# Router products taken from the residual rows, slot matrices built several tiles at a time, and two weight transfers issued behind the first gather

## What is computed

```
xn = rms_norm(x, norm_mix);  x = x + token_mixer(xn, ...)     # attention + gated linear attention
hn = rms_norm(x, norm_ffn)
g_logits = hn @ w_rg + b_rg      # 4 groups, top 1
e_logits = hn @ w_re + b_re      # 8 experts in the group, top 2
out += (silu(hn @ w_gate[e]) * (hn @ w_up[e])) * weight @ w_down[e]
x = rms_norm(x + out, norm_final)
```

## Time and profile before

| what | value |
|---|---|
| median of 3 runs | 623.91 us (623.71 to 625.61) |
| the profiled execution | 623.14 us |
| its span, first to last instruction | 621.4 us |
| granted TensorE clock, mean of the span | 0.99 |
| busy PE / DVE / ACT / POOL | 584.4 / 268.0 / 209.2 / 65.6 us |
| chain that ended last: PE / DMA / SP's queue / DVE | 76 / 11 / 5 / 5% |
| moved by DMA | 155.83 MB, 251 GB/s over the span |

### The profile page before, as it was taken

The page is one execution under the profiler, slowest core; times in us unless marked ns, Lnnn a source line. Parts: engine busy times, 40 slices in busy tenths (PEclk is TensorE's granted clock), DMA queues, the critical chain, the costliest instruction groups (busy, mean ns, idle before and its releaser), DMA issues.

```text
span 621.4 us, 8693 instructions
## 1 busy us (share of the span) xinstructions
PE 584.4 (94%) x3453; PEld 443.0 (71%) x3454; DVE 268.0 (43%) x590; ACT 209.2 (34%) x407; POOL 65.6 (11%) x108
## 2 busy tenths in 40 slices
PE   3999999999999999999999998999999998887894
PEld 3789989888688888888888874766666765553451
DVE  3647477654433657433362377312111211012247
ACT  3545466554596633422252240111111111111113
POOL 4000000000002201100000012112212211111001
PEclk9999999999999999999999999999999999889998
DMA  7476030802222222188888288899999999999994
GB/s 252 91 257 201 7 103 10 302 37 69 68 78 59 68 69 69 35 278 282 298 318 347 102 315 328 321 401 424 422 423 426 421 423 426 426 423 425 425 422 183
DMA packets 58282, 155.83 MB, mean 251 GB/s; under 512 B 8172, under 2 KB 38148, under 8 KB 45952
## 3 DMA queue, kind: packets, MB, share of 16 engines
q1 hardware_dynamic: 53392, 145.73, 61.4%
q0 software_dynamic: 4720, 9.45, 4.1%
q10 hardware_dynamic: 128, 0.09, 0.0%
HBM read 147.37 MB, written 15.75 MB: 263 GB/s over the span
## 4 chain that ended last, share of the span: by engine, by line
PE 76%; DMA 11%; SPq 5%; DVE 5%; issue 1%; POOL 1%; ACT 1%; DVEq 0%; POOLq 0%; ACTq 0%
PE bank L728 43%; PE bank L1118 11%; PE bank L1139 6%; PE bank L721 5%; SPq L492 5%; DMA slot2a<-expert_w_up 5%; DMA zt<-expert_rows 3%; PE bank L823 1%; DMA expert_rows<-y,zcol 1%; PE bank L904 1%; DMA x_in<-x 1%; PE bank L801 1%; PE bank L802 1%; PE bank L927 1%; PE bank L883 1%
## 5 line engine op out<-in xcount | busy, mean ns | idle before, releaser
L1118 PE MATMUL bank<-slots,xgT 128*64 128x256 f32 x544 | 79.9, 388 | 4.8 <-DMA slot2b<-expert_w_up 2.4
L1723 DVE TENSOR_TENSOR w_low<-w,w_high 128x1024 fp32r<-128x1024 f32 x32 | 39.2, 1225 | 75.5 <-ACT w_high L1368 75.5
L1118 PEld LDWEIGHTS bank<-slots,xgT 128*64 128x64 f32 x544 | 53.7, 139 | 22.4 <-issue 4.6
L728 PE MATMUL bank<-x_high,w_high 128*128 128x512 f32 x168 | 67.0, 399 | 1.0 <-DVE x_low L1640 1.0
L728 PE MATMUL bank<-x_high,w_low 128*128 128x512 f32 x168 | 65.6, 391 | 0.0
L728 PE MATMUL bank<-x_low,w_high 128*128 128x512 f32 x168 | 65.6, 390 | 0.0
L1368 ACT ACTIVATE w_high<-w 128x1024 fp32r<-128x1024 f32 x32 | 33.7, 1054 | 48.7 <-PE bank L728 48.7
L2013 DVE TENSOR_SCALAR y<-bank,slot_weights 128x512 f32<-128x512 f32 x14 | 10.5, 751 | 86.6 <-PE bank L1139 86.6
L728 PE MATMUL bank<-w_high,x_high 128*128 128x420 f32 x128 | 45.4, 354 | 0.0
L728 PE MATMUL bank<-w_high,x_low 128*128 128x420 f32 x128 | 45.3, 354 | 0.0
L728 PE MATMUL bank<-w_low,x_high 128*128 128x420 f32 x128 | 45.2, 353 | 0.0
(11 more groups left out here) (279 smaller groups left out, 1150.0 us busy)
## 6 DMA issues: line engine op xcount, KB each, us to landing
slots<-expert_w_gate SPq DMA_DIRECT2D x19, 1024.0 KB, 28.1
slots<-expert_w_up SPq DMA_DIRECT2D x17, 1024.0 KB, 20.5
slots<-expert_w_down SPq DMA_DIRECT2D x16, 1024.0 KB, 8.0
slot2b<-expert_w_down SPq DMA_DIRECT2D x9, 1024.0 KB, 27.3
w<-w_in SPq DMA_DIRECT2D x16, 512.0 KB, 3.7
slot2b<-expert_w_up SPq DMA_DIRECT2D x8, 1024.0 KB, 8.2
slot2b<-expert_w_gate SPq DMA_DIRECT2D x8, 1024.0 KB, 28.3
w<-w_in SPq DMA_DIRECT2D x8, 840.0 KB, 4.7
```

Source lines behind the costliest of these rows:

```text
L728: ins_ = mm(out_, stat[a_], mov[b_], start=first and q_ == 0, stop=last and q_ == 2)
L1118: ins = mm(bank[2][e * SLOTS:(e + 1) * SLOTS, m * FE:(m + 1) * FE], xgT[:, c, e * SLOTS:(e + 1) * SLOTS], gu[m][e][:, c], start=(c == 0), ...
L1723: V.tensor_tensor(wl2[:, u % 2, :], raw2[:, u % 2, :], wh2[:, u % 2, :].bitcast(F32), ALU.subtract).then_inc(s["lo_done"], 1)
```

## The change

Four things change together.

1. The router takes the residual rows themselves: `turn_x2` turns `x2` instead of `hn_st`, the gains `norm_ffn` are multiplied into `rw` once, earlier (they come in with a second small transfer at the start), and `router_out` multiplies by the row factor while it adds the bias. `normed` is still computed, for the rows that are stored, but stands later in DVE's order, and `row_squares(3)` behind the four `turned_rows` of ACT. `route(2, 3)` stands ahead of the first `token_major`.
2. `selb` is computed from the sum of the two choices ahead of `sel`, not from `sel`.
3. `first_in` is made in two instructions for all 8, `hot[k, 0]` in three (4, 3 and 1 matrices), compared with a permuted copy `dealt` of the counting row that is made once. The `keep_busy(1)` between the eight small products go, and `keep_busy(22)` becomes `keep_busy(19)`.
4. SP issues parts 11 and 20 only when POOL has issued the first gather.

```diff
@@ SP
             sp.wait_ge(s["rl_done"], 6)
-            load_part(11)
             sp.wait_ge(s["hn_out"], 16 * (ZERO_PIECES + NT))
             sp.wait_ge(s["hT_done"], 2 * NT)
+            sp.wait_ge(s["pool_step"], 1)
+            load_part(11)
             load_part(20)
@@ POOL
             first_gather(0)
+            pool.sem_inc(s["pool_step"], 1)
             first_gather(1)
@@ PE
-            def turn_hn(t):
-                pe.wait_ge(s["hn_done"], t + 1)
+            def turn_x2(t):
+                pe.wait_ge(s["x2_done"], 2 * (t + 1))
                 for c in range(KC):
-                    ins = tr(bank[2 * t + c // 4][:, (c % 4) * P:(c % 4 + 1) * P], hn_st[:, t, c * P:(c + 1) * P])
+                    ins = tr(bank[2 * t + c // 4][:, (c % 4) * P:(c % 4 + 1) * P], x2[:, t, c * P:(c + 1) * P])
...
-            for t in range(3):
-                turn_hn(t)
+            for t in range(NT):
+                turn_x2(t)
             route(0, 2)
-            turn_hn(3)
+            route(2, 3)
             token_major(0, 2, 1)
-            route(2, 3)
             route(3, 4)
...
-            keep_busy(22)
+            keep_busy(19)
...
             for k in range(2 * NT):
-                pe.wait_ge(s["hot_done"], k + 1)
+                pe.wait_ge(s["hot_done"], 1 + sum(k >= k0 for k0 in HOT_CUTS[:-1]))
                 ins = mm(bank[6][:, 0:2], hot[:, k, 0, :], first_in[:, k, :], start=(k == 0), stop=(k == 2 * NT - 1))
-                if k < 2 * NT - 1:
-                    keep_busy(1)
@@ ACT
+            for half_, gains in enumerate((norm_mix, norm_ffn)):
+                act.dma_start(g16[half_ * KC:(half_ + 1) * KC, :], gains.rearrange("(c p) -> c p", p=P)).then_inc(s["norm_in"], 16)
...
             for t in range(3):
                 row_squares(t)
-            turned_rows(0)
+            for t in range(NT):
+                turned_rows(t)
             row_squares(3)
-            turned_rows(1)
-            turned_rows(2)
             turned_logits(0, 2, 1)
-            turned_rows(3)
-            turned_logits(2, 3, 3)
+            turned_logits(2, 3, 2)
@@ DVE
+            V.tensor_copy(dealt.rearrange("p (x e l) -> p x e l", l=4, e=8), K["iota"].rearrange("p (x l e) -> p x e l", l=4, e=8)
+                          ).then_inc(s["cb_done"], 1)
...
+                V.tensor_tensor(rw[:], rw[:], bc(gcol_ffn, NG + EXPERTS), ALU.mult).then_inc(s["cb_done"], 1)
...
-                V.tensor_tensor(lg[:, t0:t1, :], bank[1 + t0][:, t0 * (NG + EXPERTS):t1 * (NG + EXPERTS)].rearrange(
-                    "p (t n) -> p t n", n=NG + EXPERTS), rb[:].unsqueeze(1).to_broadcast([P, t1 - t0, NG + EXPERTS]), ALU.add
-                    ).then_inc(s["rl_out"], 1)
+                for t in range(t0, t1):
+                    V.scalar_tensor_tensor(out=lg[:, t, :], in0=bank[1 + t0][:, t * (NG + EXPERTS):(t + 1) * (NG + EXPERTS)],
+                                           scalar=rstd2[:, t:t + 1], in1=rb[:], op0=ALU.mult, op1=ALU.add).then_inc(s["rl_out"], 1)
...
             residual(3)
-            normed(2)
             router_in(0)
             router_in(1)
-            normed(3)
+            normed(2)
             router_in(2)
             router_in(3)
+            normed(3)
...
+            link(V.tensor_tensor(tmp8, hot1, hot2, ALU.add))
+            V.tensor_tensor(selb[:].rearrange(by_group, g=NG), bc(g_hot, NE), tmp8.unsqueeze(2).to_broadcast([P, NT, NG, NE]),
+                            ALU.mult).then_inc(s["selb_done"], 1)
...
-            V.tensor_tensor(selb[:], sel[:, 0], sel[:, 1], ALU.add).then_inc(s["selb_done"], 1)
...
-            for k in range(2 * NT):
-                V.tensor_scalar(hot[:, k, 0, :].rearrange("p (x e l) -> p x e l", l=4, e=8), dealt, pf[:, 0, k:k + 1], None, ALU.is_equal)
-                V.tensor_scalar(first_in[:, k, :], K["iota"][:, 0:2], pf[:, 1, k:k + 1], K["tokval"][:, k % NT:k % NT + 1],
-                                ALU.is_equal, ALU.mult).then_inc(s["hot_done"], 1)
+            link(V.tensor_tensor(first_in, K["iota"][:, 0:2].unsqueeze(1).to_broadcast([P, 2 * NT, 2]), bc(pf[:, 1, :], 2), ALU.is_equal))
+            V.tensor_tensor(first_by_way, first_by_way.bitcast(F32), bc(K["tokval"][:, 0:NT], 2).unsqueeze(1).to_broadcast([P, 2, NT, 2]),
+                            ALU.mult)
+            for k0, k1 in zip((0,) + HOT_CUTS, HOT_CUTS):
+                V.tensor_tensor(hot[:, k0:k1, 0, :], dealt.unsqueeze(1).to_broadcast([P, k1 - k0, P]), bc(pf[:, 0, k0:k1], P),
+                                ALU.is_equal).then_inc(s["hot_done"], 1)
```

More of the change, by code:

```diff
@@ L131, in hybrid_encoder @@
         gn = sb("gn", [P, GV])
-        gcol = sb("gcol", [P, KC])
+        gcols = sb("gcols", [P, 2 * KC])
+        gcol, gcol_ffn = gcols[:, 0:KC], gcols[:, KC:2 * KC]
         row_norms = sb("row_norms", [P, 6, NT])
@@ L204, in hybrid_encoder @@
         relb, vrow = startup[0:BKT, 1700:1700 + HEADS], startup[0:HEADS, 1024:1536]
-        g8 = startup[0:KC, 1536:1536 + P]
+        g16 = startup[0:2 * KC, 1536:1536 + P]
         at_ = REST
@@ L286, in hybrid_encoder @@
         ZERO_PIECES = 2 * NT
+        HOT_CUTS = (4, 7, 8)
         arrived = {(n_, m_): sum(32 if q_ in HALVED else 16 for q_, (p_, w_, _) in enumerate(order)
@@ L732, in _ @@
             pe.wait_ge(s["ident_in"], 16)
-            pe.wait_ge(s["norm_in"], 16)
-            tr(bank[KC - 1][:, 0:KC], g8).then_inc(s["gc_done"], 1)
+            pe.wait_ge(s["norm_in"], 32)
+            tr(bank[KC - 1][:, 0:2 * KC], g16).then_inc(s["gc_done"], 1)
             for t in range(NT):
@@ L1031, in route @@
             def route(t0, t1):
+                pe.wait_ge(s["cb_done"], 7)
                 pe.wait_ge(s["hnT_outA"], t1)
@@ L1042, in token_major @@
                 pe.wait_ge(s["lt_out"], n)
-                if n == 1:
-                    pe.wait_ge(s["cb_done"], 5)
                 for t in range(t0, t1):
@@ L1079, in _ @@
             for k in range(2 * NT):
-                pe.wait_ge(s["hot_done"], k + 1)
+                pe.wait_ge(s["hot_done"], 1 + sum(k >= k0 for k0 in HOT_CUTS[:-1]))
                 ins = mm(bank[6][:, 0:2], hot[:, k, 0, :], first_in[:, k, :], start=(k == 0), stop=(k == 2 * NT - 1))
-                if k < 2 * NT - 1:
-                    keep_busy(1)
             ins.then_inc(s["first_done"], 1)
             for k in range(2 * NT):
-                pe.wait_ge(s["hot_done"], 2 * NT + k + 1)
+                pe.wait_ge(s["hot_done"], len(HOT_CUTS) + k + 1)
                 ins = mm(bank[4][:, 0:P], hot[:, k, 0, :], hot[:, k, 1, :], start=(k == 0), stop=(k == 2 * NT - 1))
@@ L1094, in slot_weights @@
                 for k in range(2 * NT):
-                    pe.wait_ge(s["hot_done"], 4 * NT + k + 1)
+                    pe.wait_ge(s["hot_done"], len(HOT_CUTS) + 2 * NT + k + 1)
                     ins_ = mm(bank[6][:, 0:P], hot[:, k, 0, :].bitcast(F32), weights_at[:, k, 1, :], start=(k == 0),
@@ L1283, in _ @@
             act.wait_ge(s["gc_done"], 1)
-            A(gcol[:], bank[KC - 1][:, 0:KC], ACT.Copy).then_inc(s["gcol_done"], 1)
+            A(gcols[:], bank[KC - 1][:, 0:2 * KC], ACT.Copy).then_inc(s["gcol_done"], 1)
             def split_high(k):
@@ L1678, in _ @@
             V.memset(unit_base, UNIT).then_inc(s["cb_done"], 1)
+            dve.wait_ge(s["cb_done"], 4)
+            dealt = K["before"]
+            V.tensor_copy(dealt.rearrange("p (x e l) -> p x e l", l=4, e=8), K["iota"].rearrange("p (x l e) -> p x e l", l=4, e=8)
+                          ).then_inc(s["cb_done"], 1)
             def maxima(i):
@@ L1923, in _ @@
             residual(3)
-            normed(2)
             router_in(0)
             router_in(1)
-            normed(3)
+            normed(2)
             router_in(2)
             router_in(3)
-            router_out(0, 2, 2)
+            normed(3)
+            router_out(0, 2, 3)
             router_out(2, 4, 6)
-            dve.wait_ge(s["rl_out"], 2)
+            dve.wait_ge(s["rl_out"], NT)
             g_lg = lg[:, :, 0:NG]
@@ L1958, in _ @@
             V.tensor_tensor(ex, v2, v1, ALU.subtract).then_inc(s["rexp_in"], 1)
+            link(V.tensor_tensor(tmp8, hot1, hot2, ALU.add))
+            by_group = "p t (g i) -> p t g i"
+            V.tensor_tensor(selb[:].rearrange(by_group, g=NG), bc(g_hot, NE), tmp8.unsqueeze(2).to_broadcast([P, NT, NG, NE]),
+                            ALU.mult).then_inc(s["selb_done"], 1)
             for k, oh in enumerate((hot1, hot2)):
-                ins = V.tensor_tensor(sel[:, k].rearrange("p t (g i) -> p t g i", g=NG), bc(g_hot, NE),
+                ins = V.tensor_tensor(sel[:, k].rearrange(by_group, g=NG), bc(g_hot, NE),
                                       oh.unsqueeze(2).to_broadcast([P, NT, NG, NE]), ALU.mult)
             link(ins)
-            V.tensor_tensor(selb[:], sel[:, 0], sel[:, 1], ALU.add).then_inc(s["selb_done"], 1)
             dve.wait_ge(s["rank_done"], 1)
@@ L1980, in _ @@
```

(9 more changed lines are left out.)

1 line of the change is left out of this document (removed).

## The result

The changed kernel takes **632.16 us** (median; 631.67 to 633.4) against 623.81 us for the kernel before on the same chip: a ratio of 1.0129, 95% interval 1.0113 to 1.0146. It is 8.35 us slower, where 621.3 us was forecast with a range that ended at 623.4. The profiled execution took 631.94 us, its span is 630.2 us.

A forecast was written before the change was run, and what follows sets the result against it. PE bounds the kernel up to 501 us, but transfers set the last 120 us. Pair 0 starts 0.8 + 0.3 + 1.75 = 2.85 us earlier, the stream gains 2.6: 623.14 to 620.5, plus 0.77 gives 621.3 us, range 620.0 to 623.4.

The forecast's parts named there:

- Router, `selb` and slot matrices: Between projections and pair 0: gains of 0.8, 0.3 and 1.75 us, so pair 0 starts 2.85 us earlier.
- the column rate: DVE's stacked slot comparisons: 1.2 ns a column and about 0.1 us fixed, 1.3 us for the three large ones.
- rival B: Slot matrices: repeated operand reads make stacking gain 0.5 us in place of 1.75; kernel 622.5 us; 4 in 100.
- The price that I took from the Trainium skill: Slot matrices: 58 cycles plus columns an instruction, 1.5 us for the sixteen, 1.4 for the five; stacking gains 0.1.
- The late store: SP's last store goes out 2.6 us later; POOL's clearing of xg ends 2.7 later, with 2 us of cover.
- rival D: POOL late: a last store over 2 us later than reckoned delays the gather one for one; 3 in 100.
- Parts 11 and 20 now come 1.35 us behind the gather's start: First gather: SP issues both parts only after the gather's 1.19 us on POOL, so behind its start.
- rival C: The two parts overtake the first gather; landing at 8.0 us costs 4.5, kernel 625.6 us; 8 in 100.
- I take 0: First gather's landing: no change, between bounds of 0.2 us gained and 4.5 lost.
- At nothing: Second small transfer, dealt copy, gains on rw and fewer keep_busy cost nothing; each uncovered at most its own 0.4 us.
- The stream's gain of 2.6: Weight stream: one hole of 3.8 us replaces 7.6 or 5.3, so all that follows comes 2.6 us earlier.
- Fewer `keep_busy`: Ahead of pair 0: clock at 1.00, gaps grow from 0.5 to about 0.9 us, at no cost.

The follow-up runs named there:

- e12: e6 with a small POOL operation behind the first gather, whose end raises the semaphore for parts 11 and 20: 622.1 us, ratio 0.9974.
- e10: e6 with the semaphore for parts 11 and 20 raised behind POOL's second gather instead of its first: 628.88 us, ratio 1.0064.
- e3: The kernel before with only the fourth edit, parts 11 and 20 held until the first gather is issued: 631.15 us, ratio 1.0115.
- e5: The kernel before with an unused tile that moves every tile behind gcol by 32 bytes per partition: 627.7 us, ratio 1.0056.
- e14: The kernel before with an unused tile of 32 columns that moves everything behind it by 128 bytes per partition: 626.62 us, ratio 1.0045.
- e6: The changed kernel with two small tiles sharing one, so the ring of weight places is back at 48640: 627.67 us, ratio 1.0055.
- e4: The changed kernel, but SP issues parts 11 and 20 only when the first gather has landed: 627.43 us, ratio 1.0052.
- e7: The changed kernel with the edits of e4 and e6 together: 624.19 us, ratio 1.0000.
- e2: The changed kernel with its fourth edit undone, parts 11 and 20 issued as in the kernel before: 630.2 us, ratio 1.0096.
- e9: e6 with parts 11 and 20 both issued early, as in the kernel before: 626.57 us, ratio 1.0039.
- e8: e7 with part 11 issued early behind the router and only part 20 held until the gather has landed: 622.57 us, ratio 0.9974.
- e13: The kernel before with the second small transfer at the start and PE's wait for it: 624.38 us, ratio 1.0001.

## Why the prediction was wrong, point by point

**Router, `selb` and slot matrices: right.** From the projections' start `selb` ends 1.04 us earlier (forecast 0.8 + 0.3 = 1.1), and from the first comparison to `gcolm` it takes 2.15 us (381.07 less 378.92; forecast 2.1 to 2.3, before 3.94). With 0.16 us lost in between, 2.67 against 2.85. The stacked comparisons took 1.35 us, where the column rate gave 1.3; rival B is out. The fixed part of the small instructions was there to be saved, as the row said. The price that I took from the Trainium skill was not all that it states: the same section adds that the measured fixed term is about 150 cycles and not 58. With it the estimate is 3.1 us for the sixteen and 1.9 for the five, so 1.2 saved; the traces have 3.6 (377.95 to 381.53) and 1.65 (378.92 to 380.57).

**The late store: right.** The last normed tile comes 2.4 us later by the same measure (2.7 forecast). POOL's clearing ends at 378.06 and POOL then waits 4.11 us for `gcolm`, so rival D is out.

**"Parts 11 and 20 now come 1.35 us behind the gather's start (1.19 on POOL, then SP)": this step failed.** I took the length of the gather's instruction as something that the raised semaphore waits for. The trace has the parts 0.13 us ahead of it, and the landing at 8.60. That is rival C in its effect, to which I gave 8 in 100, with a landing of 8.0; but C had the parts overtake from 1.35 us behind, and here they were never behind. The step after it, "I take 0" for parts that do come 1.35 us behind, was right, as e12 shows with 3.5 us at 1.40. So the arithmetic of the gather was sound and its premise, a row of 1.19 us read as an order, was not. e10 bounds the point of decision: between 0.39 us behind the start and 1.40 us, which is 0.21 behind the instruction's end.

The Trainium skill ("DMA: Bandwidth & Descriptors", "Queues, rings and completion order") says that an engine takes turns between the queues for which it has work. The landings of 8.6 to 8.9 us beside the parts are in keeping with it, without showing the turns. What e10 and e12 add is that a gather far enough ahead isn't held up at all (3.5 us), and one level with the parts takes over twice as long.

**The price of C was too small.** I had 4.5 us for the landing. Two costs come on top. PE stood idle for 3.76 us, until 390.81, and then the clock granted was 0.86 in 390 to 392.5 and 0.50 in the next 2.5 us. Windows of 2.5 us of the changed kernel:

```profile
387.50:390.00 2.50, 0.00 (x0) 0.00 (x0) 0.00 (x0) 0.00 (x0) 0.00 (x0) 1.00 0.95 384
390.00:392.50 2.50, 1.41 (x10) 1.20 (x12) 0.44 (x1) 0.92 (x2) 0.18 (x1) 0.86 0.06 23
392.50:395.00 2.50, 2.50 (x14) 1.56 (x14) 2.33 (x11) 0.96 (x1) 1.02 (x1) 0.50 0.15 20
```

So pair 0's gate and up products took 8.54 us, not 7.13 (0.50 is the lower of the two levels, 1.2 GHz). And the hole in the stream became larger than the one it replaced: in 365 to 400, e3 moved 259 GB/s and the kernel before 330, 2.5 MB less, an estimated 5.9 us at 424 GB/s. By e3 against before, the edit costs 7 us where I had 4.5.

**A term that wasn't in the sum at all: the address.** "At nothing" lists the copy, the gains and the transfers, but not that a wider tile moves every tile behind it. It costs 3.3 us in e5, 2.0 in e14, and 4.5 to 5 where it is taken out in e6. Two more pairs differ by nothing else: e4 is 3.5 us slower than e7 and e2 3.8 slower than e9, by their differences to before. By bandwidth: 195 us (from 395 to 590) at 418 for 424 GB/s is 2.8 us, and the changed kernel loses 2.87 us between its first half part (+5.73) and its read back (+8.60). In the same measure e5 loses 2.05 and e14 3.49, and the aligned e10 and e6 0.01 and -0.18 (but e3, aligned too, 1.46).

The Trainium skill has a rule for this ("DMA: Bandwidth & Descriptors", "How a descriptor splits into AXI transactions"): a transfer's descriptor is cut at 256 byte boundaries, and one that doesn't start on a boundary still starts its first piece there, with bytes that cost and aren't used. The page doesn't say whether it is the source or the target that has to start so; here only the target moved. If a whole part's row of 8 KB is one descriptor, an estimate by the page is 33 pieces for 32, 3%, for both shifts, or, counted in its beats of 32 bytes, 257 and 260 for 256, 0.4 and 1.6%. The measured losses of rate are 1.4 and 1.2%: alike, as the pieces have it, but of neither size. That it is this cutting, and not another effect of the address, was argued and not shown.

**The stream's gain of 2.6: right in direction once its premises hold, not shown in size.** e12 has both, the order and the ring's place, and takes 622.1 us, by the medians 2.6 less than before. That this is the forecast number is luck: the ratio of its five runs says 1.6 less, with an interval from 3.2 less to none, and e8 has 1.8 with a narrower one. The trace agrees with the smaller number. Measured from the projections' start, pair 0 starts 1.7 us earlier than before and the read back 1.8, so the stream did pass on what pair 0 gained; but pair 0 gained 1.7 and not 2.85. The cause stands in e12's window of 380 to 382.5 us, which also has the hole, and in PE's timeline:

```profile
380.00:382.50 2.50, 2.50 (x10) 1.71 (x11) 1.81 (x7) 0.00 (x0) 1.71 (x3) 0.51 0.11 43
```

```profile
383.81 1.68 PE L1001 MATMUL bank<-cst,onesb 128*128 128x512 bf16 x7
385.33 1.06 PE L725 MATMUL bank<-cst,xg 128*128 128x128 f32 x8
```

The clock is at 0.51 there (0.81 in the next 2.5 us), so that PE is still busy with slot products and fillers when the rows land at 384.1, and turns them only at 385.33. I had put "Fewer `keep_busy`" at nothing; in e7, where the same window has 1.00, pair 0 is 2.75 earlier. This second term at nothing was wrong in about half the cases: of the ten kernels with fewer fillers five have a clock of 0.51 to 0.82 in that window (changed, e6, e8, e10, e12), and of the six with all fillers none is under 1.00. In the 2.5 us ahead of it PE was busy for 1.41 us in e12 and for 2.45 in the kernel before, but e7, with 1.71, kept its clock. That the dip is due to the gaps left by the fillers was not tried.

**The sum.** In the two profiled executions, up to the read back: 1.85 at the start of the projections (mostly scatter, at most some 0.6 by e13's comparison) - 2.67 for the compute edits + 5.14 for the gather (8.60 less 3.46) - 0.01 between + 1.42 for the clock (the first half part against pair 0's start) + 2.87 in the stream = 8.60. That the 2.87 is all the shift's is an attribution by its size. Built up the other way, from medians against before: e10, with the order and without the shift, is 4.6 slower, and e5 adds 3.3 for the shift; that is 7.9, measured 8.35.

**What stays open.** What the shift does inside a transfer, whether removing it in the changed kernel (4.5 to 5) really gives more than adding it to the kernel before (3.3; the intervals overlap), the start's 0.6 us, where e9's other executions lose their time, why the clock dips in some executions, and where between 0.39 and 1.40 us the order turns (there is one trace on each side).

## What to carry to other kernels

In this kernel a semaphore raised behind an indirect DMA said nothing on when that DMA's rows are in the queues. Let an operation of the same engine end in between, or wait for the landing, and look in the trace which of the two issues starts first. A gather of few rows on which an engine waits wants the queues empty or itself ahead: a bulk transfer level with it cost it 5 us here, and the engine behind it some of its clock. Before costing an edit, list what it does to the addresses of the large transfer targets, not only to instructions. And before taking a match of two numbers for proof, look at the interval and at the stage that should have made it.

## What the runs showed that I had not expected

- Moving the weights' targets by 32 or 128 bytes in a partition lowers the rate of a full stream from 424 to 418 or 419 GB/s, and a kernel with no other difference from 624.4 to 627.7 us.
- `sem_inc` behind an indirect DMA fires 0.13 us before that instruction's own start in the changed kernel, and 1.11 us before the second one's in e10. Behind a POOL operation of 0.12 us it fires in time: part 11 leaves 0.21 us after the gather's instruction has ended (e12).
- One microsecond in the time of two 1 MB transfers (0.39 or 1.40 us behind the gather's start) changes its landing from 8.9 to 3.5 us; within e12 alone, the gather ahead of them takes 3.5 and the one level with them 8.6.
- Making compute faster can gain nothing, or lose: e9 has its gather 2.76 us early, meets the queues still full, and starts pair 0 no earlier; its median is 2.3 us above before.
